# Hybrid decoder layer, FP32 by split products: values in banks one to three, and two maxima ahead of the first normalisation

## The reference

```
x += 1/2 * SwiGLU_1(RMSNorm(x))                       # width 2816
h = RMSNorm(x); P = h @ w_in                          # rg_x | rg_y | q | k | v | g | low-rank gate
   A: causal conv(4) -> RG-LRU scan, * gelu(rg_y)     # width 512
   B: gated linear attention, 4 heads, dk 64, dv 128, chunks of 32
x += w_out(concat[RMSNorm(A), RMSNorm_head(B) * silu(g)])
x += CrossAttn(RMSNorm(x), memory K/V)                # 4 heads of 256, 256 memory tokens
x += 1/2 * SwiGLU_2(RMSNorm(x))
y  = RMSNorm_final(x)
```

## Time and profile before

| | |
|---|---|
| median of three runs | 2389.03 us (2386.05 to 2389.11) |
| profiled execution | 2386.58 us |
| its span | 2384.8 us, 36652 instructions |
| TensorE busy | 2344.5 us, 98% |
| VectorE busy | 1063.1 us, 45% |
| ScalarE busy | 494.6 us, 21% |
| GpSimd busy | 519.4 us, 22% |
| mean granted TensorE clock | 0.995 |

### The profile page before, as it was taken

The page is one execution under the profiler, slowest core; times in us unless marked ns, Lnnn a source line. Parts: engine busy times, 40 slices in busy tenths (PEclk is TensorE's granted clock), DMA queues, the critical chain, the costliest instruction groups (busy, mean ns, idle before and its releaser), DMA issues. The chain is left out here.

```text
span 2384.8 us, 36652 instructions
## 1 busy us (share of the span) xinstructions
PE 2344.5 (98%) x14996; PEld 2285.9 (96%) x14996; DVE 1063.1 (45%) x1696; ACT 494.6 (21%) x697; POOL 519.4 (22%) x239
## 2 busy tenths in 40 slices
PE   7999999999999999999999999999999999999998
PEld 7999999999999989899889999799999999999998
DVE  6444334444333564565542423345443344443345
ACT  4222212122211241321410211331111111111101
POOL 2444334344432000000001000022221222221111
PEclk9999999999999999999999999999999999999998
DMA  4554454354452455656668476731111111111112
GB/s 158 212 212 167 158 193 180 145 211 168 160 193 86 161 200 184 218 213 242 236 249 319 141 264 232 280 124 54 49 40 53 35 53 35 53 35 53 35 35 76
DMA packets 89475, 352.50 MB, mean 148 GB/s; under 512 B 8944, under 2 KB 16432, under 8 KB 79152
## 3 DMA queue, kind: packets, MB, share of 16 engines
q1 hardware_dynamic: 89104, 351.12, 40.3%
q10 hardware_dynamic: 288, 0.18, 0.0%
HBM read 280.54 MB, written 70.72 MB: 147 GB/s over the span
## 5 line engine op out<-in xcount | busy, mean ns | idle before, releaser
L1733 PE MATMUL ps<-a_hi,w_sb 128*128 128x384 f32 (+1 forms) x2112 | 690.7, 327 | 6.6 <-DVE a_lo L1227 4.6
L1735 PE MATMUL ps<-a_hi,w_sb 128*128 128x384 f32 (+1 forms) x2112 | 689.2, 326 | 0.0
L1734 PE MATMUL ps<-a_lo,w_sb 128*128 128x384 f32 (+1 forms) x2112 | 689.0, 326 | 0.0
L696 POOL TENSOR_TENSOR w_sb<-w_raw,w_sb 128x1024 fp32r<-128x1024 f32 x132 | 318.1, 2418 | 1063.6 <-ACT w_sb L772 1063.6
L1733 PEld LDWEIGHTS ps<-a_hi,w_sb 128*128 128x128 f32 x2112 | 397.1, 188 | 8.3 <-issue 3.6
L1734 PEld LDWEIGHTS ps<-a_lo,w_sb 128*128 128x128 f32 x2112 | 397.2, 188 | 0.0
L1735 PEld LDWEIGHTS ps<-a_hi,w_sb 128*128 128x128 f32 x2112 | 397.0, 188 | 0.0
L1310 DVE SCALAR_TENSOR_TENSOR x<-ps,x 128x384 f32<-128x384 f32 (+1 forms) x528 | 279.3, 534 | 199.5 <-PE ps L1735 199.4
L1296 DVE TENSOR_TENSOR hf<-sil,ps 128x384 f32<-128x384 f32 x132 | 70.3, 532 | 646.7 <-ACT sil L849 646.7
L1733 PE MATMUL ps<-h_hi,w_sb 128*128 128x384 f32 (+1 forms) x1056 | 344.8, 327 | 0.0
L1735 PE MATMUL ps<-h_hi,w_sb 128*128 128x384 f32 (+1 forms) x1056 | 344.2, 326 | 0.0
(11 more groups left out here) (262 smaller groups left out, 2721.1 us busy)
## 6 DMA issues: line engine op xcount, KB each, us to landing
w_sb<-split SPq DMA_DIRECT2D x148, 1024.0 KB, 5.3
split<-st_w SPq DMA_DIRECT2D x60, 1024.0 KB, 4.1
st_raw<-in_mix_tiles SPq DMA_DIRECT2D x60, 512.0 KB, 5.9
w_raw<-in_ffn_gate SPq DMA_DIRECT2D x44, 512.0 KB, 3.7
w_raw<-in_ffn_up SPq DMA_DIRECT2D x44, 512.0 KB, 4.5
w_raw<-in_ffn_down SPq DMA_DIRECT2D x44, 512.0 KB, 4.3
kc<-in_cache_k SPq DMA_DIRECT2D x5, 1024.0 KB, 7.9
kc<-in_cache_v SPq DMA_DIRECT2D x4, 1024.0 KB, 9.1
```

Source lines behind the costliest of these rows:

```text
L696: nc.gpsimd.tensor_tensor(w_lo_sb[:, slot_, :], raw[:, slot_, :], w_hi_sb[:, slot_, :].bitcast(F32), ALU.subtract)\
L1733: nc.tensor.matmul(dst, w_h, x_h, start=start, stop=False)
L1734: nc.tensor.matmul(dst, w_h, x_l, start=False, stop=False)
L1735: return nc.tensor.matmul(dst, w_l, x_h, start=False, stop=stop)
```

## The change

Three edits go together for the values: they are accumulated in banks 1 to 3, copied from there, and the tiles 4, 5 and 6 of the stage, whose banks 0, 1 and 2 are now left by the previous stage, the first and the second copy, wait for `evicted` to reach t - 4 rather than t - 3. Tile 7 (bank 3) waits for the third copy as before. In cross-attention of groups 0 and 1 VectorE takes the maxima of tiles 0 and 1 and then divides tiles 0 and 1; group 2 keeps its order.

```diff
             def evict_values(n):
...
-                    nc.vector.tensor_copy(vt[0:w, i, :], ps[0:w, i, :]).then_inc(evicted, (1, 1, 2)[i])
+                    nc.vector.tensor_copy(vt[0:w, i, :], ps[0:w, 1 + i, :]).then_inc(evicted, (1, 1, 2)[i])
...
                 norm_head(*beside, ())
-                for t in range(2):
-                    if n == 2:
-                        sample_max(t)
-                    row_max(n, t)
-                    normalise(n, t)
                 if n < 2:
+                    row_max(n, 0)
+                    row_max(n, 1)
+                    normalise(n, 0)
+                    normalise(n, 1)
                     row_max(n, 2)
                     normalise(n, 2)
                     for t in range(TT):
                         out_lo(n, t)
                 else:
+                    for t in range(2):
+                        sample_max(t)
+                        row_max(n, t)
+                        normalise(n, t)
                     sample_max(2)
...
-            def tile(t, k4, group, hi, lo, N, norm_of=None, half_of=None):
+            def tile(t, k4, group, hi, lo, N, norm_of=None, half_of=None, bank_after=None):
...
                     pe.wait_ge(x_added, DOWNS - 3 + t)
+                elif bank_after is not None:
+                    pe.wait_ge(evicted, bank_after)
                 else:
                     pe.wait_ge(evicted, t - 3)
...
-                tile(t, t % RING, t // RING, hi, lo, N, norm_of, half_of)
+                tile(t, t % RING, t // RING, hi, lo, N, norm_of, half_of, t - 4 if kind == "gla" and j < 7 else None)
...
-                token_tiles(FIRST["gla", n], xh[n], xl[n], NS[n], between_values)
+                token_tiles(FIRST["gla", n], xh[n], xl[n], NS[n], between_values, banks=1)
```

## The result

The changed kernel takes 2380.36 us (median of 7 runs, 2378.25 to 2381.93), the kernel before on the same chip 2388.19 us (7 runs, 2385.9 to 2392.03). The ratio is 0.9967 with an interval of 0.9957 to 0.9976: 7.8 us faster, between 5.7 and 10.3. The forecast was 2382 us.

What follows compares the result with a forecast made beforehand. TensorE, busy for 98% of the span, was taken as the bound. Value stages 4.48 us (1.60 of it clock) plus softmax 2.76 us make 7.24 us, off 2389.03 us: 2381.8, rounded 2382 us; range 2377.5 to 2387 us.

Steps and rivals of the forecast that it cites:

- Group 0, the stall: Value stage of group 0: tile 4 no longer waits for the first value eviction and starts 1.65 us earlier.
- Group 0, the clock: Tiles 4 and 5 of group 0: the low clock behind the removed stall goes too, 1.60 us.
- rival A: Low-clock term of group 0 absent, stalls go as worked out: 5.64 us gained, 2383.4 us; chance 0.28.
- Group 1: Value stage of group 1: stall ahead of tile 4 goes, 1.23 us gained, no low clock to win.
- Group 2: Value stage of group 2: the removed 0.68 us becomes a longer wait of the spread for VectorE's reciprocal; gain 0.
- Softmax: Cross-attention of groups 0 and 1: maxima of tile 1 ahead of tile 0's normalisation, 1.38 us each, 2.76 us together.
- delay of tile 0: Cross-attention: tile 0's normalisation ends 1.4 us later, costed at nothing, with 0.95 us of cover left before TensorE's first transposes.
- stall of tile 1: Cross-attention of group 0: TensorE's wait of 1.45 us ahead of tile 1's transposes shrinks to some 0.2 us.
- 0.16 us ahead of tile 2: Cross-attention of group 0: TensorE's stall of 0.16 us ahead of tile 2's transposes stays.
- B: Another wait replaces the removed one, one of the two parts lost: 2.76 to 2.9 us gained, about 2386 us; chance 0.15.
- C: Neither part gains, order bound by the reciprocal in every group and by ScalarE in the softmax: 2389 us; chance 0.05.
- D: Slower: the clock falls in new stretches of TensorE's narrow work, 3.3 us each, 2396.6 us with four; chance 0.04.

Runs made afterwards that it cites:

- the stall put back: Changed kernel with tiles 4 to 6 of group 0 again waiting for one eviction more; 2383.24 us against 2387.62 for the kernel before, ratio 0.998.
- The two parts alone: Kernel before with only the value edits (2384.08 us, ratio 0.9983), and kernel before with only the new softmax order (2385.07 us, ratio 0.9991).
- the third profile of before: Kernel before, nothing changed, profiled a third time; 9.97 us from tile 4 to the spread of group 0.
- the maxima alone: Kernel before with only the new softmax order in groups 0 and 1; 2385.07 us against 2387.62, ratio 0.9991.
- the four built on the changed kernel: Changed kernel with group 2's reciprocal ahead of the scans (2378.45 us), third sample pair's maxima earlier (2379.97), both (2378.47), or last recurrence scan done twice (2383.64).
- both additions: Changed kernel with group 2's reciprocal ahead of the scans and the third sample pair's maxima earlier; 2378.47 us against 2388.19 for the kernel before, ratio 0.9958.

## Why the prediction was right, point by point

**Group 0, the stall.** 1.65 us by the prediction, 1.65 by the section with the stall put back. Tile 4 was to start at 870.68 and the spread at 879.08; with the 0.16 us by which this execution runs ahead from M on, they came at 870.67 and 879.08.

**Group 0, the clock.** The term was mis-sized. It was taken as 1.60 us in every execution; it is 1.6 us in three of six, so by these six it is worth 0.8 in the mean. The forecast and rival A were put as two cases of which one is true. They are two kinds of execution of the same kernel: where the kernel before had the low clock there, the gain is the forecast's, otherwise A's. The doubt was rightly placed, "the trace can't decide".

**Group 1.** 1.23 us forecast, 1.24 measured. **Group 2.** No gain and a wait of 0.9 us forecast; 137.38 to 137.41 us and 0.95 measured.

**Softmax.** 1.38 us for each group forecast, 1.37 measured. The delay of tile 0 was hidden with 1.1 us of cover, 0.95 forecast. The stall of tile 1 did not shrink to 0.2 but to nothing, while the gain was the same to 0.01 us, so the 0.2 was within the reading of starts. The 0.16 us ahead of tile 2 stayed.

**The sum.** 7.24 us against 7.26 from M to C2 in the pair of traces, which both had the clock term to win. The medians give 7.8, somewhat more than the 5.64 + 0.8 = 6.4 that the sections and half a clock term make; 6.4 lies within the interval (5.7 to 10.3). The two parts alone gave 3.5 and 2.6 us, 6.1 together. The medians can't settle whether more than 6.4 is won. So the stalls were forecast by their mechanism, but that the median came nearer to the forecast's 7.24 than to 6.4 is luck as far as the runs show, and no evidence for the clock term.

**Rivals.** B and C did not come: neither part was lost. D did not come as a slower kernel, but its sign, a stretch of low clock in a new place, did show in the first profile of the changed kernel, at 1197 and near 1580. The first is nothing new: stretches between 1195 and 1218 are in every one of the 14 profiles, with or without the change, 3.4 us long or 6.8 in all (1.7 or 3.4 us lost), and some have two separate ones instead of one of double length, as the third profile of before. The second is open. Around the two waits near 1580 the clock is low in two of the four profiles of before, and over all in two of the seven profiles with the old softmax order and in all seven with the new one (those of the changed kernel, the maxima alone, the stall put back and the four built on the changed kernel). From the second wait to the last weight matmul it takes 780.25 to 780.30 us without it and 781.8 to 783.3 with it. No run tests whether the change has a part in that. The medians show no such loss: the gain is no smaller than the sections make it.

**What the prediction left out.** It costed the transfers at nothing. That held for the changed tiles, but one of the four profiles of before lost 1.4 us to late weights at 1259 and 1273. The profile of both additions lost 0.5 us in the same way. Such a loss is of the size of a term of this sum and says nothing on the change.

## What to carry to other kernels

A stall of the engine that bounds the kernel is worth its idle time only if what is next in its list is ready: read the timeline up to the next wait, take the distance to its releaser as the cover, and expect the gain to end there, as in group 2. When a gain of a few microseconds is to be read, compare sections between fixed instructions of the traces; with no stretch of low clock and no late transfer in them they agree to about a tenth of a microsecond or better where whole runs of one kernel spread over four to six. In a ring of buffers, one that is free when a long producer hands over to the next lets the consumer start without waiting for the producer; here it hid a delay of 1.65 us in group 0.

## What the runs showed of the hardware

The granted clock of TensorE fell behind the vt stalls of 1.5 us in three of six executions and behind those of 2.1 and 2.5 us in all four cases seen, and stayed up behind those of 1.1 us in all of five. Elsewhere it fell behind the one wait of 1.87 us, never behind 14 waits of 1.45 us in cross-attention, and in nine of 14 profiles at or shortly behind the first of two waits near 1580 (1.10 and 1.37 us, 2.2 us apart). Between 1195 and 1218 it fell in all 14 while TensorE was busy throughout. So at the same place of the same kernel it falls in one execution and not in another, and neither the length of a wait nor the busy share tells by itself whether it will.

Ahead of the tail the stretches at the lower level were 3.4 or 6.8 us long, never between, so a TensorE that is busy loses 1.7 or 3.4 us to one, and less where it would have stood still anyway. The spread of whole runs of one kernel, 3.7 and 6.1 us among seven, is of the size of two to four losses of 1.7 us.

The Trainium skill, "TensorE: Matmul & The Clock Gate", Part 1, says that the place of a change of level varies from run to run; by that rule the term is in some executions only, and the traces agree: 10.0 us for the 48 matmuls behind the stall in three executions, 8.4 us in three.
